# Rotary embedding of the first block's queries and keys: from a TensorE matmul to four VectorE operations, and an earlier place for four turns in its attention

## The chip, the cores and the metric

One core of one Trainium2 chip runs the whole program. The metric is the device time of one execution in microseconds (us), as the median of several runs. PE is TensorE, DVE is VectorE, ACT is ScalarE, POOL is GpSimd, and SP is the queue that loads weights.

## The reference, cut to what matters

The model has two blocks one behind the other. The change touches the first block only, which has two layers on 512 tokens. Each layer projects the normed input, rotates queries and keys, and runs three attention branches, a gated recurrence and a convolution beside each other:

```
q   = apply_rope(q.reshape(B, T, N_HEADS, HEAD_DIM), cos, sin)
k_c = apply_rope(kvr(k_c), cos, sin)      # likewise k_s and k_w
...
u1, u2 = jnp.split(uf, 2, axis=-1)        # the halves of a head: 32 and 32
out = jnp.concatenate([u1 * cos - u2 * sin, u2 * cos + u1 * sin], axis=-1)
```

## The kernel before, in words

Activations lie with features on the 128 partitions and the 512 tokens in the free dimension. A projection is a list of strips. A strip makes 128 output features: 8 chunks of the input times 128x128 weights, each chunk as three matmuls of a high and a low part (`three`, L949 to L951), into one PSUM bank. Strips use two banks in turn, so strip n waits until DVE has emptied the bank of strip n-2 (`taken`).

Weights come by SP in pieces of four chunks. ACT rounds a piece to its high part (`split_to`, L1334), POOL subtracts to get the low part (L2452), and PE waits for that. ACT takes its instructions in a fixed order: for strip n it first splits the pieces of strips n+1 and n+2, as far as `last_of(n) + SPLIT_RING` allows (4 pieces on), and then does its work on strip n and on strip n-1 (`evac`, `side`).

Part B of each layer has the strips k_c, v_c, q0, q1, c00, q2, c01, q3, d0, k_s, c10, v_s, c11, k_w, d1, v_w, g, z0, z1, z2 in this order; z3 is run inside the attention that follows. The c and d strips are the small matrices that compress keys and values (62 columns). Their weights are not split, and a c strip has 4 pieces, so ACT splits the weights of the strip behind it only when it comes to the c strip itself, and by then it has done `side` of the strip two before the c strip. So the weights of q2 (behind c00) wait for ACT's copy of the rotated q0, those of q3 (behind c01) for that of q1, and those of v_s (behind c10) for that of q3. Those of k_s are split at q3, behind ACT's copy of the rotated q2.

The seven strips k_c, q0 to q3, k_s and k_w of each layer (14 in all) are rotated. DVE scales the bank by the norm into a buffer (L1773, `evac`). PE multiplies the buffer by the constant matrix `rot`, which swaps the halves of each head and negates one (L1068, `rotate`, into bank 3). DVE multiplies that by the sines (L1990), the buffer by the cosines (L1995) and adds both (L1997). ACT copies the sum to its high part (L1476), and DVE subtracts to get the low part (L2001). For k_c DVE builds the blocks to be compressed instead (L2051). Between these DVE does the taps of the convolution (L2234), a fixed number behind each strip (`TAPS`).

In the attention NSA that follows, tiles come in pairs (two heads), two pairs make a group, and step s does on PE: the scores of group s (`scores`, L1161 and L1167), the values of group s-2 (`values`, L1198 and L1201), and the turns (transposes) of the probabilities of group s-1 (`turn`, L1188). POOL has scaled these probabilities before, and ACT or DVE copies each turned tile out of PSUM (L1540, L2123). The 9 pairs of one head column add up in bank 6. The first pair of the next column may start only when DVE has taken bank 6 (`output`, L2132). Pairs 9 and 27 of the 36 of a layer are the first of a column and the second of their group.

Of the kernel before, what the change touches and what calls it, by code (L numbers as in the profile page):

```python
# [22 lines left out]
ALU = mybir.AluOpType  # L23
# [3 lines left out]
P = 128  # L27
T = 512
NT = T // P
# [3 lines left out]
HD = 64  # L33
N_CMP = 31
CMP_PAD = 32
# [177 lines left out]
N_PARAM = _at  # L213


CONSTS = [("ident", P), ("ones", P), ("halves", P), ("rot", P), ("causal", T), ("cmp_mask", NT * CMP_PAD), ("cmp_any", 1), ("inv_freq", 1)]
EXTRA = [("rotc", P), ("band", 384), ("cos2d", T), ("sin2d", T), ("cos1d", T), ("sin1d", T), ("cosc", T), ("sinc", T),
         ("colmask", GRID)]
CONST_AT, EXTRA_AT = {}, {}
# [9 lines left out]
def build(nc, stream, x_in, mem_in, pos_in, par_in, const_in, extra_in, lruw_in, bias_in, out, counts):  # L229
# [5 lines left out]
    with ExitStack() as ctx:  # L235
# [43 lines left out]
        sin_t = sb("sin_t", [P, T])  # L279
# [31 lines left out]
        def C(name):  # L311
            a, w = CONST_AT[name]
            return consts[:, a:a + w]
# [5 lines left out]
        ident = C("ident")  # L319
# [200 lines left out]
        def rope_units(s):  # L520

            if s.kind in ("q", "qn"):
                return [(C("rot") if s.kind == "q" else None, s.idx)]
            if s.kind in ("k_s", "kn"):
                return [(C("rot") if s.kind == "k_s" else None, 4)]
            if s.kind in ("qr", "kr"):
                return [(None, 5 + s.idx if s.kind == "qr" else 9)]
            if s.kind == "k_w":
                return [(C("rot"), 5)]
            if s.kind == "k_c":  # L530
                return [(C("rot"), "cmp")]
            if s.kind == "uq":
                return [(extra("rotc"), ("latent", s.idx))]
            if s.kind == "krope":
                return [(extra("rotc"), "krope")]
            return []
# [149 lines left out]
        def in_group(groups, s):  # L686
            return groups[s] if 0 <= s < len(groups) else []
# [98 lines left out]
        def RAW(n):  # L786

            return raws[n % 4] if STRIPS[n].part[0] == "AB" else raw[n % 2]
# [157 lines left out]
        def _(pe):  # L946
# [110 lines left out]
            def rotate(n):  # L1057
                s = STRIPS[n]
                for u in s.units:
                    rot, _ = UNITS[u]  # L1060
                    if rot is None:
                        continue

                    pe.wait_ge(*after("latent_raw" if s.kind == "uq" else "strip_taken", n))
                    if u >= 1:

                        pe.wait_ge(*after("rope_taken", u - 1))
                    pe.matmul(bank[3][:, :], rot, rope_src(s), start=True, stop=True).then_inc(*mark("rotated", u))  # L1068
# [56 lines left out]
            def attend(part):  # L1125
# [102 lines left out]
                for s in range(steps_of(part)):  # L1228
                    if part[0] == "C2" and s < len(groups):
                        latent_scores(groups[s])  # L1230
                    else:
                        for pair in in_group(groups, s):
                            scores(pair)
                    if part[0] == "NSA" and s + 1 < len(GATE_CHUNKS):
                        for _ in range(GATE_CHUNKS[s + 1]):
                            next(begun[LAST_GATE[part[1]]])
                    if 0 <= s - len(groups) < 3:
                        drain(part, steps[s - len(groups)])
                    if PAIRS[part[0]] == 2:
                        for pair in in_group(groups, s - value_lag):  # L1240
                            values(pair)
                    for pair in in_group(groups, s - turn_lag):
                        for t in pair:
                            turn(t)
                    if PAIRS[part[0]] == 1:
                        for pair in in_group(groups, s - value_lag):
                            values(pair)
                    for i in moments_of(part, s):
                        for stage in between.get(i, ()):
                            extra_stage(*stage)  # L1250
# [426 lines left out]
        def _(dve):  # L1677
# [296 lines left out]
            def rope(n):  # L1974

                s = STRIPS[n]
                for u in s.units:
                    dst = UNITS[u][1]
                    src, swap = RAW(n), UNITS[u][0] is None
                    dve.wait_ge(*after(f"swapped{u % 2}" if swap else "rotated", u))  # L1980
                    turned, rt = (swapped[u % 2], swapped[u % 2]) if swap else (bank[3], tmp(2))
                    table = {"qn": "2d", "kn": "2d", "qr": "1d", "kr": "1d", "krope": "c"}.get(s.kind)
                    cos, sin = tables_of(s)
                    if table is not None:

                        dve.wait_ge(*after("tables_in_" + table, "sin"))
                        if table == "2d":
                            dve.wait_ge(*after("extra_in", "colmask"))
                    to = rr2[s.idx] if s.kind == "uq" else rr if dst != "krope" else krb
                    ins = dve.tensor_tensor(rt[:, :], turned[:, :], sin[:, :], ALU.mult)  # L1990
                    if s.kind == "uq":
                        ins.then_inc(*mark("rope_taken", u))
                    else:
                        settle(ins)
                        dve.tensor_tensor(to[:, :], src[:, :], cos[:, :], ALU.mult).then_inc(*mark("rope_taken", u))  # L1995
                    dve.wait_ge(*after("rope_taken", u))
                    dve.tensor_tensor(to[:, :], to[:, :], rt[:, :], ALU.add).then_inc(*mark("roped", u))  # L1997
                    dve.wait_ge(*after("roped", u))
                    if isinstance(dst, int):
                        dve.wait_ge(*after("roped_high", u))  # L2000
                        settle(dve.tensor_tensor(side_lo[:, dst, :], rr, side_hi[:, dst, :].bitcast(F32), ALU.subtract))  # L2001
                    elif dst == "cmp":
                        cmp_blocks(s.layer, 0)
# [465 lines left out]
def shape_constants():  # L2469

    f = np.float32
    d = np.arange(P)
    swap_sign = np.where(d % HD < 32, -1, 1).astype(f)[:, None]
    rot = np.zeros((P, P), f)
    for o in range(P):
        rot[o + 32 if o % HD < 32 else o - 32, o] = -1 if o % HD < 32 else 1
    q, x = d[:, None], np.arange(T)[None, :]
    n = np.arange(CMP_PAD)[None, None, :]
    t = (P * np.arange(NT))[None, :, None] + d[:, None, None]
    named = dict(  # L2480
        ident=np.eye(P, dtype=f), ones=np.ones((P, P), f), halves=(d[:, None] // HD == d[None, :] // HD).astype(f),
        rot=rot,
        causal=np.where(x - 384 <= q, 0, NEG).astype(f),
        cmp_mask=np.where((n < N_CMP) & (S_CMP * n + L_CMP - 1 <= t), 0, NEG).astype(f).reshape(P, -1),
        cmp_any=(d[:, None] >= L_CMP - 1).astype(f),
        inv_freq=(f(10000.0) ** (-(2 * (d % 32)).astype(f) / f(HD))).astype(f)[:, None],
    )
    pos = np.arange(T)
    inv64 = (f(10000.0) ** (-np.arange(0, 64, 2, dtype=f) / f(64))).astype(f)
    inv32 = (f(10000.0) ** (-np.arange(0, 32, 2, dtype=f) / f(32))).astype(f)  # L2490
    a1 = pos.astype(f)[None, :] * inv64[d % 32][:, None]
    fr = d % 32
    a2 = np.where(fr[:, None] < 16, (pos // GRID)[None, :], (pos % GRID)[None, :]).astype(f) * inv32[fr % 16][:, None]
    ac = pos[None, :].astype(f) * inv32[d % 16][:, None]
    rotc = np.zeros((P, P), f)
    for o in range(P):
        rotc[o + 16 if o % 32 < 16 else o - 16, o] = -1 if o % 32 < 16 else 1
    near = []
    for i in (0, 1):
        qc, kc = near_columns(i)  # L2500
        c0 = np.clip(qc - SPAN // 2, 0, GRID - SPAN)[SPAN // 2 * (d // GRID) + d % (SPAN // 2)][:, None]
        near.append(np.where((kc[None, :] >= c0) & (kc[None, :] < c0 + SPAN), 0, NEG))
    xb = np.arange(384)[None, :]
    extra = dict(rotc=rotc, band=np.where(np.abs(xb - P - q) <= 128, 0, NEG).astype(f),
                 cos2d=np.cos(a2).astype(f), sin2d=(swap_sign * np.sin(a2)).astype(f), cos1d=np.cos(a1).astype(f), sin1d=(swap_sign * np.sin(a1)).astype(f),
                 cosc=np.cos(ac).astype(f), sinc=np.sin(ac).astype(f),
                 colmask=np.concatenate(near, 1).astype(f))
    return (np.concatenate([named[k] for k, _ in CONSTS], 1), np.concatenate([extra[k] for k, _ in EXTRA], 1))

# [115 lines left out]
```

## Time and profile before

| What | us |
|---|---|
| Three runs: median (lowest to highest) | 2230.45 (2222.82 to 2232.63) |
| The profiled execution: its own time | 2232.77 |
| The profiled execution: span from the first to the last instruction | 2231.0 |
| PE busy in the span | 2151.1 |
| DVE busy | 1182.0 |
| ACT busy | 1014.1 |
| POOL busy | 1023.5 |

The span leaves 1.8 us of the execution's own time outside. Busy times are averages over stages with different limits. The mean granted clock of TensorE is 0.988 of its full speed.

### The profile page before, as it was taken

The numbers are of one execution on the slowest core, as the hardware profiler recorded it, in microseconds if no ns is written. First come the engines' busy times: TensorE is split into PE (matmuls) and PEld (weight loads), VectorE is DVE, ScalarE is ACT, GpSimd is POOL, SyncE is SP. The second block draws the span as 40 slices with busy tenths as digits, with TensorE's granted clock in tenths as the row PEclk, the third lists the DMA queues.
The fourth block names the chain that finished last, engine by engine and source line by source line (L and its number), as shares of the span: only waits on it lengthen the run. The fifth ranks groups of instructions, "written<-read, shape, count | busy, mean of one in ns | idle before, by whom it ended". The sixth has DMA issues, their size and how long they took to land.

```text
span 2231.0 us, 32894 instructions
## 1 busy us (share of the span) xinstructions
PE 2151.1 (96%) x11928; PEld 1747.1 (78%) x11928; DVE 1182.0 (53%) x2470; ACT 1014.1 (45%) x2020; POOL 1023.5 (46%) x937
## 2 busy tenths in 40 slices
PE   8999989999998899999999999999989999999997
PEld 6778767887876788768888888888757878888886
DVE  5997664389876546785562212234466654211222
ACT  6542455466246553585453323333356554322332
POOL 4433455444246544354345545554345525554553
PEclk9999989999999999999999999999999999999998
DMA  5334102333320233203233333333120413333332
GB/s 167 87 93 138 29 11 67 104 91 93 126 64 7 67 86 110 71 21 89 84 89 96 94 111 97 92 102 123 40 61 28 132 46 104 95 95 99 99 94 67
DMA packets 106895, 187.87 MB, mean 84 GB/s; under 512 B 12016, under 2 KB 22768, under 8 KB 106608
## 3 DMA queue, kind: packets, MB, share of 16 engines
q1 hardware_dynamic: 101136, 178.67, 27.7%
q10 hardware_dynamic: 5600, 7.11, 1.0%
q8 instruction: 97, 1.59, 0.3%
q14 instruction: 62, 0.51, 0.1%
HBM read 181.01 MB, written 2.10 MB: 82 GB/s over the span
## 4 chain that ended last, share of the span: by engine, by line
PE 86%; DVE 7%; ACT 2%; issue 2%; POOL 2%; DMA 0%; SPq 0%; DVEq 0%; ACTq 0%
PE bank L949 24%; PE bank L951 23%; PE bank L950 23%; PE bank L1188 4%; PE bank L1201 3%; PE bank L1167 2%; DVE bank L2234 1%; PE bank L956 1%; POOL temp L2406 1%; PE bank L1019 1%; PE bank L1146 1%; POOL w_lo L2452 1%; ACT temp L1529 1%; PE bank L1068 1%; PE bank L977 0%
## 5 line engine op out<-in xcount | busy, mean ns | idle before, releaser
L2452 POOL TENSOR_TENSOR w_lo<-w_raw,w_hi 128x512 fp32r<-128x512 f32 (+3 forms) x618 | 823.7, 1339 | 976.7 <-ACT w_hi L1334 976.5
L949 PE MATMUL bank<-op_hi,w_hi 128*128 128x512 f32 x1840 | 732.5, 398 | 11.5 <-POOL w_lo L2452 4.6
L951 PE MATMUL bank<-op_hi,w_lo 128*128 128x512 f32 x1840 | 719.5, 391 | 0.0
L950 PE MATMUL bank<-op_lo,w_hi 128*128 128x512 f32 x1840 | 719.2, 391 | 0.0
L1334 ACT ACTIVATE w_hi<-w_raw 128x512 fp32r<-128x512 f32 (+2 forms) x634 | 385.5, 617 | 685.1 <-PE bank L951 681.7
L949 PEld LDWEIGHTS bank<-op_hi,w_hi 128*128 128x128 f32 x1840 | 347.0, 189 | 96.0 <-issue 15.7
L950 PEld LDWEIGHTS bank<-op_lo,w_hi 128*128 128x128 f32 x1840 | 347.2, 189 | 74.0 <-issue 4.1
L951 PEld LDWEIGHTS bank<-op_hi,w_lo 128*128 128x128 f32 x1840 | 346.9, 189 | 73.1
L1773 DVE TENSOR_TENSOR temp<-bank,rstd 128x512 f32<-128x512 f32 x139 | 96.1, 691 | 368.4 <-PE bank L951 350.8
L949 PE MATMUL bank<-side_hi,w_hi 128*128 128x512 f32 (+1 forms) x628 | 233.1, 371 | 2.6 <-DVE side_lo L1872 1.4
L951 PE MATMUL bank<-side_hi,w_lo 128*128 128x512 f32 (+1 forms) x628 | 230.9, 368 | 0.0
L950 PE MATMUL bank<-side_lo,w_hi 128*128 128x512 f32 (+1 forms) x628 | 230.8, 368 | 0.0
L1854 DVE TENSOR_TENSOR x_t<-bank,x_t 128x512 f32<-128x512 f32 x80 | 55.3, 691 | 315.8 <-PE bank L951 315.6
L1529 ACT ACTIVATE temp<-temp,small 128x256 f32<-128x256 f32 (+3 forms) x288 | 166.2, 579 | 41.7 <-DVE small L2076 24.7
L2234 DVE SCALAR_TENSOR_TENSOR bank<-conv_area,par,bank 128x512 f32<-128x512 f32 x232 | 174.9, 754 | 6.8
L1188 PE MATMUL bank<-consts,temp 128*128 128x128 f32 x800 | 127.7, 285 | 31.6 <-POOL temp L2406 8.4
L1188 PEld LDWEIGHTS bank<-consts,temp 128*128 128x128 f32 x800 | 86.3, 142 | 71.6 <-issue 35.8
L949 PEld LDWEIGHTS bank<-side_hi,w_hi 128*128 128x128 f32 x628 | 118.4, 189 | 24.9 <-DVE side_lo L1872 2.7
L950 PEld LDWEIGHTS bank<-side_lo,w_hi 128*128 128x128 f32 x628 | 118.4, 189 | 19.5 <-issue 0.5
L951 PEld LDWEIGHTS bank<-side_hi,w_lo 128*128 128x128 f32 x628 | 118.4, 189 | 19.5
L2408 POOL TENSOR_SCALAR temp<-temp,small,consts 128x512 f32<-128x512 f32 (+2 forms) x128 | 85.2, 680 | 101.7 <-DVE small L2100 101.6
L2406 POOL TENSOR_SCALAR temp<-temp,small,gates 128x128 f32<-128x128 f32 (+3 forms) x128 | 76.6, 613 | 62.0 <-DVE small L2100 62.0
(286 smaller groups left out, 2431.7 us busy)
## 6 DMA issues: line engine op xcount, KB each, us to landing
w_raw<-in_weights SPq DMA_DIRECT2D x620, 256.0 KB, 2.7
w_raw<-in_weights SPq DMA_DIRECT2D x32, 192.0 KB, 2.3
temp<-temp SPq DMA_DIRECT2D x40, 64.0 KB, 2.0
x_t<-in_x SPq DMA_DIRECT2D x8, 256.0 KB, 5.3
conv_area<-in_mem ACTq DMA_DIRECT2D x2, 1024.0 KB, 5.4
conv_area<-in_bias ACTq DMA_DIRECT2D x1, 2048.0 KB, 7.6
out_y<-ybuf SPq DMA_DIRECT2D x8, 256.0 KB, 2.1
w_raw<-in_weights SPq DMA_DIRECT2D x10, 128.0 KB, 2.1
```

Of the source, the lines that this page charges most:

```text
L949: pe.matmul(dst, w[0], m[0], start=start, stop=False)
L950: pe.matmul(dst, w[0], m[1], start=False, stop=False)
L951: return pe.matmul(dst, w[1], m[0], start=False, stop=stop)
L1188: ins = pe.transpose(bank[t["turn"]][:, P * b:P * b + P], E[a % E_RING][:, P * b:P * b + P], ident)
L1201: ins = pe.matmul(dst, t["pv"][b], PT[a % PT_RING][:, P * b:P * b + P], start=t["start"] and b == 0, stop=t["stop"] and last)
L1334: act.activation(w_hi[:, j, 0:m * w], w_raw[:, p % RAW_RING, 0:m * w], ACT.Copy).then_inc(*mark("weights_high", p))
L1529: act.activation(e, e, ACT.Exp, bias=m, scale=-1.0, accum_out=total).then_inc(*mark("exps", a))
L1773: return dve.tensor_tensor(dst, strip_bank(n)[0:rows, 0:s.cols], f[0:rows, 0:s.cols], ALU.mult)
L2234: settle(dve.scalar_tensor_tensor(out=acc[:, c, :] if j == CONV_K - 1 else run, in0=u_conv[:, c, j:j + T], scalar=w, in1=run, op0=ALU.mult ...
L2406: ins = pool.tensor_scalar(e, e, total[:, r:r + 1], t["gate"], ALU.mult, ALU.mult)
L2408: ins = pool.tensor_scalar(e, e, total[:, r:r + 1], C("ones")[:, 0:1], ALU.mult, ALU.mult)
L2452: pool.tensor_tensor(w_lo[:, j, 0:n], w_raw[:, p % RAW_RING, 0:n], w_hi[:, j, 0:n].bitcast(F32), ALU.subtract).then_inc(*mark("weights_spl ...
```

## The change

Part one: the 14 rotations of part B leave PE. DVE multiplies by the sines itself, in four operations of 32 rows that read the other half of the head; its wait for PE is gone, and the matrix `rot` (128 columns of the constants, loaded at the start) is gone too. The products are the same numbers. The rotations of the second block stay as they were.

Part two: in NSA, where the second pair of a group is the first of a head column (pairs 9 and 27, so twice in a layer), PE does all four turns of the next group between the values of the first pair and those of the second, and not behind both.

```diff
-CONSTS = [("ident", P), ("ones", P), ("halves", P), ("rot", P), ("causal", T), ...
+CONSTS = [("ident", P), ("ones", P), ("halves", P), ("causal", T), ...
...
@@ rotate (PE)
-                    if rot is None:
+                    if rot is None or s.part[0] == "B":
                         continue
...
@@ attend (PE)
+                    to_turn = [t for pair in in_group(groups, s - turn_lag) for t in pair]
                     if PAIRS[part[0]] == 2:
-                        for pair in in_group(groups, s - value_lag):
+                        for i, pair in enumerate(in_group(groups, s - value_lag)):
+                            if part[0] == "NSA" and i == 1 and pair[0]["first"]:
+                                while to_turn:
+                                    turn(to_turn.pop(0))
                             values(pair)
-                    for pair in in_group(groups, s - turn_lag):
-                        for t in pair:
-                            turn(t)
+                    for t in to_turn:
+                        turn(t)
...
@@ rope (DVE)
-                    src, swap = RAW(n), UNITS[u][0] is None
-                    dve.wait_ge(*after(f"swapped{u % 2}" if swap else "rotated", u))
+                    src, swap, by_rows = RAW(n), UNITS[u][0] is None, s.part[0] == "B"
+                    if not by_rows:
+                        dve.wait_ge(*after(f"swapped{u % 2}" if swap else "rotated", u))
...
-                    ins = dve.tensor_tensor(rt[:, :], turned[:, :], sin[:, :], ALU.mult)
+                    if by_rows:
+                        for a in range(0, P, HD):
+                            low_rows, high_rows = slice(a, a + 32), slice(a + 32, a + HD)
+                            dve.scalar_tensor_tensor(out=rt[low_rows, :], in0=src[high_rows, :], scalar=-1.0, in1=sin_t[high_rows, :], op0=ALU.mult, op1=ALU.mult)
+                            ins = dve.tensor_tensor(rt[high_rows, :], src[low_rows, :], sin_t[low_rows, :], ALU.mult)
+                    else:
+                        ins = dve.tensor_tensor(rt[:, :], turned[:, :], sin[:, :], ALU.mult)
```

## Rows read from the trace of the kernel before

**Rows 1.** The page: busy time by engine, its share of the span, instructions.
```profile
PE 2151.1 (96%) x11928; PEld 1747.1 (78%) x11928; DVE 1182.0 (53%) x2470; ACT 1014.1 (45%) x2020; POOL 1023.5 (46%) x937
```

**Rows 2.** Windows: part B behind v_c in both layers (PE, PEld, DVE, ACT, POOL).
```profile
148.70:240.00 91.30, 89.51 (x453) 72.86 (x451) 74.46 (x122) 24.00 (x40) 29.44 (x23) 1.00 0.39 119
555.86:647.20 91.34, 89.48 (x453) 72.87 (x451) 74.42 (x121) 24.00 (x40) 29.44 (x23) 1.00 0.39 118
```

**Rows 3.** The rotation's line (two records each), and PE's timeline around the first.
```profile
L1068 PE MATMUL bank<-temp,consts x28: 590/592/697, 148.7 to 617.4; 128*128 128x512 f32 x28
...
148.25 0.39 PE L950 MATMUL bank<-op_lo,w_hi 128*128 128x512 f32 x1
148.47 0.39 PE L951 MATMUL bank<-op_hi,w_lo 128*128 128x512 f32 x1
...
149.80 0.40 PE L950 MATMUL bank<-op_lo,w_hi 128*128 128x512 f32 x1
```

**Rows 4.** Timeline of all engines from the end of q1 to q2.
```profile
160.76 0.69 DVE L1773 TENSOR_TENSOR temp<-bank,rstd 128x512 f32<-128x512 f32 x1 [0.42 <-PE bank L951]
...
161.55 0.69 DVE L1990 TENSOR_TENSOR temp<-bank,sin_t 128x512 f32<-128x512 f32 x1
162.27 0.69 DVE L1995 TENSOR_TENSOR temp<-temp,cos_t 128x512 f32<-128x512 f32 x1
...
163.72 0.63 ACT L1476 ACTIVATE side_hi<-temp 128x512 fp32r<-128x512 f32 x1 [14.13 <-DVE temp L1997]
164.26 1.13 ACT L1334 ACTIVATE w_hi<-w_raw 128x512 fp32r<-128x512 f32 x2
...
166.42 0.47 PE L949 MATMUL bank<-op_hi,w_hi 128*128 128x512 f32 x1 [0.48 <-POOL w_lo L2452]
```

**Rows 5.** DVE's timeline: a strip of 24 rows, and three operations with no wait between.
```profile
222.35 0.68 DVE L1773 TENSOR_TENSOR temp<-bank,rstd 24x512 f32<-24x512 f32 x1
...
546.52 0.68 DVE L2018 TENSOR_TENSOR temp<-bank,temp 128x512 f32<-128x512 f32 x1
547.11 0.69 DVE L2019 SCALAR_TENSOR_TENSOR bank<-temp,bank 128x512 f32<-128x512 f32 x1
```

**Rows 6.** DVE's timeline: operations on 64 rows without a wait, in overlapping windows.
```profile
152.27 0.58 DVE L2051 TENSOR_TENSOR temp<-temp,par 64x248 f32<-64x248 f32 x1
152.77 1.15 DVE L2051 TENSOR_TENSOR temp<-temp,par 64x248 f32<-64x248 f32 x2
153.35 1.06 DVE L2051 TENSOR_TENSOR temp<-temp,par 64x248 f32<-64x248 f32 x2
```

**Rows 7.** Timeline: DVE's slack at q2 and q3, ACT's splits for k_s and v_s.
```profile
172.25 0.69 DVE L1773 TENSOR_TENSOR temp<-bank,rstd 128x512 f32<-128x512 f32 x1 [0.96 <-PE bank L951]
...
179.65 1.14 ACT L1334 ACTIVATE w_hi<-w_raw 128x512 fp32r<-128x512 f32 x2
...
182.17 0.69 DVE L1773 TENSOR_TENSOR temp<-bank,rstd 128x512 f32<-128x512 f32 x1 [1.63 <-PE bank L951]
...
191.00 1.13 ACT L1334 ACTIVATE w_hi<-w_raw 128x512 fp32r<-128x512 f32 x2
```

**Rows 8.** PE's timeline where NSA's first head column ends, and DVE's output.
```profile
276.73 0.61 PE L1201 MATMUL bank<-temp,vz 128*64 128x128 f32 x8
...
277.41 0.69 DVE L2132 TENSOR_TENSOR ybuf<-bank,ybuf 128x512 f32<-128x512 f32 x1 [0.25 <-PE bank L1201]
...
278.20 0.29 PE L1198 MATMUL bank<-temp,vcz 128*64 128x128 f32 x1 [0.87 <-issue]
...
280.30 0.45 PE L1167 MATMUL bank<-side_hi 64*128 64x384 f32 x2
```

**Rows 9.** Timeline: a wait of PE; windows behind it (the clock third from last).
```profile
326.98 2.13 PE L1188 MATMUL bank<-consts,temp 128*128 128x128 f32 x10 [2.52 <-POOL temp L2406]
...
329.00:330.00 1.00, 1.00 (x9) 0.95 (x10) 0.58 (x5) 0.98 (x5) 0.32 (x1) 0.50 0.00 0
...
331.00:332.00 1.00, 1.00 (x14) 1.00 (x12) 0.28 (x2) 0.16 (x2) 0.88 (x2) 0.59 0.00 0
```

More of the change, by code:

```diff
@@ L213 @@
 N_PARAM = _at
-CONSTS = [("ident", P), ("ones", P), ("halves", P), ("rot", P), ("causal", T), ("cmp_mask", NT * CMP_PAD), ("cmp_any", 1), ("inv_freq", 1)]
+CONSTS = [("ident", P), ("ones", P), ("halves", P), ("causal", T), ("cmp_mask", NT * CMP_PAD), ("cmp_any", 1), ("inv_freq", 1)]
 EXTRA = [("rotc", P), ("band", 384), ("cos2d", T), ("sin2d", T), ("cos1d", T), ("sin1d", T), ("cosc", T), ("sinc", T),
@@ L522, in rope_units @@
             if s.kind in ("q", "qn"):
-                return [(C("rot") if s.kind == "q" else None, s.idx)]
+                return [("rows" if s.kind == "q" else None, s.idx)]
             if s.kind in ("k_s", "kn"):
-                return [(C("rot") if s.kind == "k_s" else None, 4)]
+                return [("rows" if s.kind == "k_s" else None, 4)]
             if s.kind in ("qr", "kr"):
@@ L528, in rope_units @@
             if s.kind == "k_w":
-                return [(C("rot"), 5)]
+                return [("rows", 5)]
             if s.kind == "k_c":
-                return [(C("rot"), "cmp")]
+                return [("rows", "cmp")]
             if s.kind == "uq":
@@ L2473, in shape_constants @@
     swap_sign = np.where(d % HD < 32, -1, 1).astype(f)[:, None]
-    rot = np.zeros((P, P), f)
-    for o in range(P):
-        rot[o + 32 if o % HD < 32 else o - 32, o] = -1 if o % HD < 32 else 1
     q, x = d[:, None], np.arange(T)[None, :]
@@ L2481, in shape_constants @@
         ident=np.eye(P, dtype=f), ones=np.ones((P, P), f), halves=(d[:, None] // HD == d[None, :] // HD).astype(f),
-        rot=rot,
         causal=np.where(x - 384 <= q, 0, NEG).astype(f),
```

## The prediction

> **What bounds the kernel now.** I read the page first. PE is busy for 96% of the span, DVE for 53% [rows 1]. By that reading work should go from PE to DVE. But these are averages, so I took the windows of part B, where the 14 rotations are: DVE works 74.5 of 91.3 us there and PE 89.5 [rows 2]. Both layers have the same picture within 0.1 us. DVE has 17 us free in a layer, and the next question is where.
>
> The timeline shows it [rows 4]. DVE waits 0.42 us for q1 to end (160.76), rotates q0 from 161.55, and ACT, which had been idle for 14.13 us because the next instruction in its fixed order is the copy of the rotated q0, makes the copy at 163.72. Only then does it split the weights of q2 (164.26). POOL makes the low part, and PE starts q2 at 166.42, after a wait for it. So behind a c strip the rotation on DVE is what PE waits for: DVE, ACT, POOL, PE in a chain. The same chain leads from the rotated q2 to the weights of k_s (split at 179.65) and from q3 to those of v_s (191.00) [rows 7]. Ahead of q2 DVE has almost no free time.
>
> **What leaves PE.** A rotation is two records of 592 ns that overlap. Between the last L951 before it and the second matmul of the next strip lie 149.80 - 148.47 = 1.33 us, where two steps of 0.23 us would be 0.45 [rows 3]. So it costs 0.88 us, and 14 are 12.3 us. That is the gain if PE sets the pace.
>
> **What comes to DVE.** L1990 takes a step of 162.27 - 161.55 = 0.72 us [rows 4]. Four operations of 32 rows take its place. Fewer rows save nothing: 24 rows by 512 take 0.68 us, as 128 rows do [rows 5]. The negating form with a number for its scalar (L2019) takes 0.69 us too. No row before has two inputs from SBUF in that form; I take 0.69 us and leave 0.76 us as a bound.
>
> The step from one operation to the next is in doubt. Where nothing is waited for it can be 547.11 - 546.52 = 0.59 us, 0.09 less than the duration [rows 5]. In L2051 the steps are 0.50 and then 0.58 us, at durations of 0.56 to 0.58 [rows 6]. The 0.50 lies between two operations on the same rows; the 0.58 comes where the output changes to the other 64 rows. In the new series the rows of input and output change at every operation. By the first rows the four take 3 x 0.60 + 0.72 = 2.52 us, so 1.80 us more than now; by the second 3 x 0.70 + 0.72 = 2.82 us, 2.10 more. I take 2.10, since L2051 is the nearer row, and keep 1.80 and, for contention or a slower form, 2.40 as bounds.
>
> The Trainium skill (VectorE: DVE Perf Modes, Two Vector instructions with no wait between them) says that a Vector instruction whose input or output starts in another group of 32 partitions than the one before is held until all earlier ones have finished. By it the series takes the longer step; L2051 agrees.
>
> **The walk through part B (layer 0; layer 1 has the same steps).** I follow how late each thing is. Up to q2 two rotations (k_c, q0) add 2 x 2.10 = 4.2 us. DVE saves 0.1 us twice, where it now waits for L1068 behind the scaling, and the 0.42 us wait for PE is used up. So ACT's copy and q2 are 3.6 us late (170.0). PE had gained 1.75 us by then (two rotations) and stands idle for 6 to 7 us.
>
> The rotation of q1 adds 2.2; DVE's slack of 0.96 us at q2 [rows 7] goes; the scaling of q2 is 4.8 late. The rotation of q2 adds 2.2, and the split for k_s is 7.0 late. k_s began 2 us after its weights were ready, so it is 5.0 late. Ahead of q3's scaling DVE had 1.63 us free [rows 7]; the rotation of q3 adds 2.1; the split for v_s is 7.5 late and v_s itself 6.9, after 0.6 us of its own slack. From here on the gains and losses on PE count. The rotation of k_w goes (0.88 less). DVE, some 8 us late by then with the rotations of k_s and k_w, delays the strips behind it by up to 0.6 us. Then it has time to catch up (few taps, no rotation). So z2 and the end of part B are 6.7 us late in each layer. With 1.80 for 2.10 the walk gives 4.9, with 2.40 it gives 8.4. The same walk without the new costs comes within 1.1 us of the starts in the trace, at every strip.
>
> The idle time before q2 may cost more. Behind the wait of 2.52 us that ends at 326.98 the granted clock is 0.50 at 329 and 0.59 in the window from 331, and full before and behind [rows 9]: about 3.3 us at the lower level (1.2 GHz), which lose 1.6 us. If q2 runs so, the scaling of q2 waits for PE, which adds 0.4 us in the walk; k_s has cover, because DVE is later still. I add 0.4 in each layer. Part one in all: 2 x 7.1 = +14.2 us.
>
> The shorter constants (64 KB at the start) I cost at nothing: the first strips run on other transfers.
>
> **Part two.** After the last values of the column (about 277.3) PE waits for DVE's output (277.41 to 278.10), does the values of the next pair from 278.20, then two turns with a wait for a copy, and reaches the next scores at 280.30 [rows 8]. With the turns first, two of them fill the wait; the third needs ACT's copy of the first, the fourth DVE's copy of the second, which comes behind the output: 278.1 + 0.3 = 278.4. The values then run from 278.6 to 279.5 and the scores start at 279.6, 0.7 us sooner. In the other place of the layer the wait is also 0.87 us. Four places give 2.8 us at most; nothing is the lower bound. I take 2.8: the turns also release DVE's and ACT's copies. What is queued behind the earlier turns is the pair's values; ACT's third copy waits for them, and they come sooner as well.
>
> **Sum.** 14.2 - 2.8 = +11.4 us. Against the profiled execution 2232.77 + 11.4 = 2244.2. That execution lies 2.3 us above the median of the runs, so for the median 2230.45 + 11.4 = 2241.9, say 2242. About 0.5% (11.2 us) is what a measurement of this kernel can tell from no change; the forecast lies on that edge.
>
> **The rivals.**
> - *Shorter steps on DVE* (1.80 us a rotation, or slack that the walk doesn't see): 2 x 4.9 - 2.8 = +7, so 2237. For it: three operations at 0.60 us [rows 5]. Against it: rows change here. Chance 0.25.
> - *PE's clock.* PE will stand idle ahead of q2 (about 6.9 us), k_s (about 3 to 4) and v_s (1 to 3). If the lower level holds for 6 us and not 3.3, q2 loses 3 us and passes 1.5 of it on; if v_s too runs slowly, there is no cover and 1.6 us or more go straight to the end. That makes 8.9 to 11 us a layer, less 2.8: +15 to +19, so 2246 to 2250. For it: the longest idle time is more than twice that of [rows 9]. Chance 0.25. The Trainium skill (TensorE: Matmul & The Clock Gate, Part 1) says that the array's clock is granted by how busy it has lately been and falls to half after idling; the windows agree, and by it each long gap is paid for.
> - *The rotation is hidden and PE sets the pace* (the other side): DVE's 17 us of free time in a layer [rows 2] would swallow 7 x 2.1 = 14.7. Then 12.3 + 2.8 = 15 us are gained, 2215. It decides for this one if ACT's copy is not in front of the splits; the wait of 14.13 us that ends with DVE's add [rows 4] speaks against it. Half of it, with delays only ahead of q2, would be about 2226. Chance 0.05.
> - *The turns gain nothing* (POOL's scaling or DVE is late instead): +14, so 2244.5; this one lies within the forecast's own range.
>
> **The numbers.** The forecast has 0.45, with a range of its own from 2239 to 2246. The cases below and above it have 0.25 each, the hidden rotation 0.05. The range 2231 to 2250 leaves out the last and the worst of the clock. Slower by over 0.5% (above 2241.6): the upper half of the forecast (0.26) and the clock (0.24), 0.50. Faster by over 0.5% (below 2219.3): 0.03. The rest is 0.47.
>
> **What would show it.** In the profile after: no L1068 on the constants in part B; in its place 56 operations of 32x512 with a mean near 690 ns and starts 0.70 us apart (0.60: the second case). PE's wait for w_lo before q2 grows from 0.48 to 6 or 7 us, and new ones stand before k_s and v_s. The windows of part B are 6 to 8 us longer in each layer with DVE at nearly the same share. The granted clock behind q2's start tells the third case. In NSA, L1198 has no wait of 0.87 us in two of its places in a layer, and four L1188 stand before it. I am wrong if q2 starts sooner than 168, or if part B is not longer.

## The result, and the profile after

The changed kernel takes 2247.78 us (median of four runs, 2247.19 to 2249.88). The kernel before, run beside it, took 2229.34 us (four runs, 2222.82 to 2232.63). The ratio is 1.0093, with a 95% interval from 1.0076 to 1.0109. So the change costs 18.4 us where 11.4 were forecast. The direction held, and 2247.8 lies inside the wide range (2231 to 2250) but outside the forecast's own (2239 to 2246): 18.4 us lies where the rival of PE's clock stood (+15 to +19). The profiled execution took 2249.88 us, 17.1 more than that of before; its mean granted clock is 0.982, that of before 0.988.

The page first. PE lost 28 instructions and 5 us, DVE gained 42 and 33 us. The span grew all the same: PE is busy for less time in a longer span. This answers to [rows 1].

```profile
PE 2145.9 (95%) x11900; PEld 1745.9 (78%) x11900; DVE 1214.8 (54%) x2512; ACT 1013.3 (45%) x2020; POOL 1022.7 (45%) x937
```

The windows of part B behind v_c, from the same event to the same event as in [rows 2] (columns as there, the granted clock third from last):

```profile
148.51:251.42 102.91, 88.41 (x439) 73.75 (x437) 90.55 (x143) 23.55 (x40) 29.64 (x23) 0.92 0.35 105
561.71:664.43 102.72, 88.24 (x439) 73.72 (x437) 90.37 (x142) 23.54 (x40) 29.65 (x23) 0.92 0.36 105
```

Both layers grow, by 11.6 and 11.4 us. DVE now works 90.5 of 102.9 us, more than PE's 88.4. The clock was 1.00 here before and is 0.92 now.

The timeline of the first rotation (k_c) and of POOL. The four operations and then the two behind them:

```profile
149.49 1.29 POOL L2462 TENSOR_TENSOR w_lo<-w_raw,w_hi 128x512 fp32r<-128x512 f32 x1 [1.43 <-ACT w_hi L1337]
149.51 1.81 DVE L1997 SCALAR_TENSOR_TENSOR temp<-temp,sin_t 32x512 f32<-32x512 f32 x1
...
151.34 0.68 DVE L1998 TENSOR_TENSOR temp<-temp,sin_t 32x512 f32<-32x512 f32 x1
...
152.03 0.69 DVE L1997 SCALAR_TENSOR_TENSOR temp<-temp,sin_t 32x512 f32<-32x512 f32 x1
```

The first operation takes 1.81 us, where the others take 0.69. It starts 0.02 us behind an operation of POOL and ends 0.54 us after that one's end (151.32 against 150.78). Its line and the line of the 64-row operations, in part B of layer 0, show one such long operation each (durations in ns: shortest, median, longest):

```profile
L1997 DVE SCALAR_TENSOR_TENSOR temp<-temp,sin_t x14: 679/686/1814, 149.5 to 228.2; 32x512 f32<-32x512 f32 x14
...
L2061 DVE TENSOR_TENSOR temp<-temp,par x16: 561/572/1550, 154.9 to 194.5; 64x248 f32<-64x248 f32 x16
```

In the kernel before, the same view has a longest of 583 ns for the 64-row line, and one operation in L1995 of 1024 ns (median 692). So 1.13 and 0.98 us come in and 0.33 go, in both layers alike. The first of the second series of eight 64-row operations is long too, by 0.27 us, and it lies beside POOL as well:

```profile
188.72 2.79 POOL L2462 TENSOR_TENSOR w_lo<-w_raw,w_hi 128x512 fp32r<-128x512 f32 x2 [8.61 <-ACT w_hi L1337]
189.56 0.84 DVE L2061 TENSOR_TENSOR temp<-temp,par 64x248 f32<-64x248 f32 x1
```

That series takes 5.56 us in all, and took 4.29: the chain loses 1.27 us there, not 0.98.

Next the stretch that answers to [rows 4], from the rotation of q0 to q2:

```profile
163.72 0.68 DVE L1997 SCALAR_TENSOR_TENSOR temp<-temp,sin_t 32x512 f32<-32x512 f32 x1
164.41 0.68 DVE L1998 TENSOR_TENSOR temp<-temp,sin_t 32x512 f32<-32x512 f32 x1
165.10 0.69 DVE L1997 SCALAR_TENSOR_TENSOR temp<-temp,sin_t 32x512 f32<-32x512 f32 x1
165.80 0.68 DVE L1998 TENSOR_TENSOR temp<-temp,sin_t 32x512 f32<-32x512 f32 x1
166.52 0.69 DVE L2005 TENSOR_TENSOR temp<-temp,cos_t 128x512 f32<-128x512 f32 x1
...
167.97 0.63 ACT L1479 ACTIVATE side_hi<-temp 128x512 fp32r<-128x512 f32 x1 [18.57 <-DVE temp L2007]
168.51 1.13 ACT L1337 ACTIVATE w_hi<-w_raw 128x512 fp32r<-128x512 f32 x2
...
170.67 0.77 PE L949 MATMUL bank<-op_hi,w_hi 128*128 128x512 f32 x1 [6.91 <-POOL w_lo L2462]
171.23 0.63 PE L950 MATMUL bank<-op_lo,w_hi 128*128 128x512 f32 x1
```

The starts lie 0.69 and 0.70 us apart. The chain DVE, ACT, POOL, PE is there as before, and PE waits 6.91 us. The second matmul of q2 takes 0.63 us, not 0.39. The two other waits that the walk foresaw, at k_s and at v_s:

```profile
190.19 0.47 PE L949 MATMUL bank<-op_hi,w_hi 128*128 128x512 f32 x1 [2.42 <-POOL w_lo L2462]
...
203.30 0.77 PE L949 MATMUL bank<-op_hi,w_hi 128*128 128x512 f32 x1 [3.90 <-POOL w_lo L2462]
```

And the windows around q2 and v_s. The clock falls while PE stands idle and is at the lower level (1.2 GHz) when the strip begins:

```profile
164.00:166.00 2.00, 0.00 (x0) 0.00 (x0) 1.96 (x4) 0.00 (x0) 0.00 (x0) 0.65 0.85 289
166.00:168.00 2.00, 0.00 (x0) 0.00 (x0) 1.87 (x3) 0.03 (x1) 0.00 (x0) 0.50 0.05 17
...
172.00:174.00 2.00, 2.00 (x6) 1.55 (x5) 1.94 (x4) 0.26 (x1) 0.00 (x0) 0.50 0.49 176
174.00:176.00 2.00, 2.00 (x8) 1.61 (x8) 1.92 (x4) 0.00 (x0) 0.00 (x0) 0.79 0.00 0
...
204.00:206.00 2.00, 2.00 (x7) 1.52 (x6) 1.91 (x5) 0.26 (x1) 0.38 (x1) 0.50 0.60 183
206.00:208.00 2.00, 2.00 (x6) 1.61 (x5) 1.94 (x3) 0.00 (x0) 0.00 (x0) 0.50 0.04 13
208.00:210.00 2.00, 2.00 (x8) 1.53 (x8) 1.21 (x2) 1.25 (x3) 0.02 (x1) 0.76 0.00 0
```

Summed over windows of 1 us, 17.1 us of part B run at the lower level in each layer, and none did before.

Last, the place in NSA that answers to [rows 8]: four transposes now stand ahead of the pair's values, and the wait of 0.87 us is gone.

```profile
287.02 0.44 PE L1188 MATMUL bank<-consts,temp 128*128 128x128 f32 x2
287.17 0.69 DVE L2142 TENSOR_TENSOR ybuf<-bank,ybuf 128x512 f32<-128x512 f32 x1 [0.24 <-PE bank L1201]
...
287.72 0.72 PE L1188 MATMUL bank<-consts,temp 128*128 128x128 f32 x2 [0.26 <-POOL temp L2416]
...
288.37 0.32 PE L1198 MATMUL bank<-temp,vcz 128*64 128x128 f32 x1
...
289.39 0.45 PE L1167 MATMUL bank<-side_hi 64*128 64x384 f32 x2
```

From the output's start to the next scores it takes 289.39 - 287.17 = 2.22 us, and took 280.30 - 277.41 = 2.89.

**Where the 17.1 us of the profiled executions lie.** Part B holds +23.0. From its end to the first output residual behind NSA the changed kernel is 5.5 us shorter in layer 0 and 1.5 in layer 1 (-7.0): in NSA of layer 0 the kernel before had 20.5 us at the lower level, the changed one 10.2. The block behind has +1.3 (one stretch at the lower level that before lacks). So nearly all of the cost is in part B. Layer 1, where both kernels have 10.2 us at the lower level in NSA, shows what the turns give without the clock: 1.5 us. The rest of the 5.5 us in layer 0 is the clock.

### The profile page after: what moved, and what is told of

It is laid out like the page before. It is cut to its first block, busy times and chain, and to the rows that moved or that the text cites. A ratio compares the mean times of both kernels' runs of the same rounds, so it can differ in the third digit from the quotient of the medians.

```text
span 2248.1 us, 32865 instructions
## 1 busy us (share of the span) xinstructions
PE 2145.9 (95%) x11900; PEld 1745.9 (78%) x11900; DVE 1214.8 (54%) x2512; ACT 1013.3 (45%) x2020; POOL 1022.7 (45%) x937
## 4 chain that ended last, share of the span: by engine, by line
PE 84%; DVE 9%; ACT 2%; issue 2%; POOL 1%; DMA 0%; SPq 0%; DVEq 0%; ACTq 0%
PE bank L949 23%; PE bank L951 23%; PE bank L950 23%; PE bank L1188 4%; PE bank L1201 3%; PE bank L1167 2%; DVE bank L2244 1%; PE bank L956 1%; DVE temp L2061 1%; POOL temp L2416 1%; PE bank L1146 1%; DVE temp L1997 1%; DVE temp L1998 0%; DVE temp L1776 0%; DVE temp L2005 0%
```

## The experiments

To compare runs without the clock's chance elsewhere, I measured one stretch of each trace: from the start of DVE's scaling of v_c to that of z2, in layer 0. It is 90.75 us in the kernel before and 102.36 in the changed one. The last column names what PE waits for only where it isn't the low part of the weights.

| Kernel | Stretch | At the lower level in part B, layer 0 | Wait of PE at q2, k_s, v_s |
|---|---|---|---|
| before | 90.75 | 0 | 0.48, none, none |
| changed | 102.36 | 17.1 | 6.91, 2.42, 3.90 |
| e1, rows alone | 101.64 | 17.1 | 6.91, 2.42, 2.25 |
| e2, turns alone | 90.73 | 0 | as before |
| e3, two gaps filled | 99.86 | 6.8 | 1.70, 3.71, none |
| e4, splits ahead | 102.82 | 17.1 | none, 2.78, 2.89 (both for DVE) |
| e5, all on rows 0 to 31 | 99.80 | 13.6 | 6.50, 2.02, 3.61 |
| e6, k_c by PE | 98.25 | 10.3 | 4.26, 2.42, 2.26 |
| e7, only k_s and k_w by rows | 89.34 | 0 | 0.48, none, none |
| e8, three gaps filled | 99.03 | 0 | 1.70, 1.06, 2.11 |

### The two parts by themselves

e1 is the changed kernel with the turns back in their old place. e2 is the kernel before with the turns moved:

```diff
+                    to_turn = [t for pair in in_group(groups, s - turn_lag) for t in pair]
...
+                            if part[0] == "NSA" and i == 1 and pair[0]["first"]:
+                                while to_turn:
+                                    turn(to_turn.pop(0))
```

> The rotations by rows alone, the turns as before. Theory 1 (VectorE's longer rotation sets the starts of q2, k_s and v_s, and the clock falls in the gaps): part B 11.5 us longer in each layer as in the changed kernel, in all +19 to +23 us against the kernel before, so slower than the changed kernel by the 3 us of the turns. Rival: the loss comes partly from the moved turns (copies held up in the ring); then this run is less slow than the changed kernel, +15 or less.

> The moved turns alone, rotations on TensorE. Theory 1: -0.7 us at each of four places, -2.8 us in all (-0.13%), possibly 1.7 us more or less where a stretch at the lower clock moves. Rival (the turns gain nothing, or hold up the values): 0 to +3 us.

Measured (before: 2228.93, 15 runs): e1 2251.55 us, ratio 1.0102 (1.0088 to 1.0117); e2 2229.18 us, ratio 0.9998 (0.9989 to 1.0007). The rows are the whole loss. By the medians the turns alone give nothing. But the mean granted clock of e2's eleven runs is 0.9884, that of before 0.9899. At the same clock e2 is shorter: at 0.988 2229.49 against 2232.36 us (four runs each), at 0.989 2226.98 (four) against 2230.78 (three). So at one clock the turns give 2.9 to 3.8 us, and the clock took it back. e1 says the same: it lacks only the turns, its mean clock is that of the changed kernel (0.983), and it takes 3.8 us longer. e10 below tests it again.

### The clock: idle matmuls in PE's gaps

e3 fills PE's waits behind c00 and c10, e8 also the one behind the second product of the compressed keys, ahead of k_s. The matmuls write a bank that nobody reads.

```diff
+                        if STRIPS[n].kind == "cmp2" and STRIPS[n].idx in (0, (0,)):
+                            warm(3, 3)
+                        if STRIPS[n].kind == "cmp1":
+                            warm(3, {(0, 0): 6, (1, 0): 2}.get(STRIPS[n].idx, 0))
```

This is e8. e3 has the last two lines alone, with 6 and 3. The numbers say how many matmuls stand in each gap.

> The changed kernel with idle matmuls on TensorE behind c00 (6) and c10 (3) of each layer, into a bank that nobody reads, so that the gaps ahead of q2 and v_s are filled. Theory 1 with the clock: q2 starts when it did (170.7), the clock stays full, q2 no longer passes 0.7 us on and v_s no longer loses 2.8 us: 3.5 us a layer, 7 us in all below the changed kernel. Rival (the clock costs nothing because VectorE is later still): no change within 2 us, and the excess of part B over the walk is VectorE's own.

> The changed kernel with idle matmuls of TensorE in all three gaps (six behind c00, three behind the second product of the compressed keys ahead of k_s, two behind c10). The matmuls compute nothing. If what is left above the walk of 7 us a layer is the clock, no stretch at the lower level stands behind q2, k_s or v_s, and the time falls a further 2 to 5 us below that with two gaps filled: 2239 to 2242. If VectorE's lateness alone sets the strips, filling the third gap changes nothing: 2243 to 2245.

Measured: e3 2243.93 us, ratio 1.0070 (1.0056 to 1.0084). e8 2245.02 us beside a before of 2227.00, ratio 1.0077 (1.0061 to 1.0094). Both are a few us shorter than the changed kernel (ratio 1.0093), and both miss: e3 should have gained 7 us and gains 3.9, e8 should have come to 2239 to 2242 and be below e3. By the time alone e8 fits the rival, that DVE's lateness sets everything. The traces tell why. In e3 the clock fell at the gap ahead of k_s that I had left open. PE reaches it sooner and waits 3.71 us there; in the changed kernel it waits 2.42 us and the clock doesn't fall:

```profile
188.01 0.77 PE L949 MATMUL bank<-op_hi,w_hi 128*128 128x512 f32 x1 [3.71 <-POOL w_lo L2464]
```

```profile
186.00:188.00 2.00, 0.00 (x0) 0.02 (x1) 1.92 (x3) 0.98 (x2) 1.46 (x2) 0.56 0.17 64
188.00:190.00 2.00, 1.99 (x5) 1.61 (x6) 1.99 (x3) 0.00 (x0) 1.32 (x1) 0.50 0.32 122
```

In e8 nothing of part B runs at the lower level, in either layer. This is the whole of part B, from the same events as above:

```profile
148.51:248.17 99.66, 93.51 (x462) 74.13 (x460) 90.62 (x143) 23.53 (x40) 29.70 (x23) 1.00 0.36 109
```

```profile
170.75 0.47 PE L949 MATMUL bank<-op_hi,w_hi 128*128 128x512 f32 x1 [1.70 <-POOL w_lo L2466]
...
189.62 0.47 PE L949 MATMUL bank<-op_hi,w_hi 128*128 128x512 f32 x1 [1.06 <-POOL w_lo L2466]
...
202.74 0.47 PE L949 MATMUL bank<-op_hi,w_hi 128*128 128x512 f32 x1 [2.11 <-POOL w_lo L2466]
```

The strips still start late (q2 21.9 us behind the scaling of v_c in both), so the idle matmuls took nothing from the chain. What is left, 99.03 - 90.75 = 8.3 us a layer, is the cost without the clock. The clock's share in the changed kernel is 102.36 - 99.03 = 3.3 us. It can be split: q2's own scaling, and with it k_s and v_s, come 0.65 us sooner in e8 (counted from the scaling of v_c, k_s starts at 40.76 and not 41.41), and the other 2.7 us arise behind the start of v_s. What e8 gained in part B, it lost in part in NSA: 27.3 us at the lower level in both layers' NSA against 20.5 in the changed kernel.

### ACT's order

The prediction said that ACT is idle because the copy of the rotated strip stands ahead of the next split. e4 lets ACT split up to three strips ahead in part B.

```diff
+                        if step[1][0] == "B":
+                            split_ahead(n, most)
                         split_to(min(last_of(n + 2), last_of(n) + SPLIT_RING, most))
```

> The changed kernel, but ScalarE splits the weights of up to three strips ahead in part B, before it waits for the rotated strip. Theory 1 (the weights' split behind ScalarE's wait for the rotation is the link): the waits for w_lo ahead of q2, k_s and v_s go, part B gets back most of its 11.5 us; 2225 to 2232 in all. Rival (VectorE is saturated, 74.5 + 14.7 of 85 us, and the emptying of the banks sets the pace): the waits for w_lo turn into waits for VectorE's scaling, and no more than 8 us come back, 2240 or more.

Measured: 2252.29 us, ratio 1.0105 (1.0086 to 1.0123), no faster than the changed kernel. q2 does start sooner, at 167.36, without a wait. PE now waits for DVE's scaling instead:

```profile
162.04 5.56 PE L1019 MATMUL bank<-temp,w_raw 128*128 128x62 f32 x32 [2.35 <-DVE temp L1786]
...
180.59 0.61 PE L949 MATMUL bank<-op_hi,w_hi 128*128 128x512 f32 x1 [2.48 <-DVE temp L1786]
```

```profile
204.79 0.80 PE L949 MATMUL bank<-op_hi,w_hi 128*128 128x512 f32 x1 [2.89 <-DVE temp L1786]
```

So ACT's order is where the lateness enters PE in the changed kernel, but without it PE is late all the same. DVE is busy for 65.7 of the 72 us from 147 to 219, and whoever asks it next waits. My theory that this order is the binding link fell; the rival, a full DVE, holds for the most part. The run isn't a clean test, though: the earlier splits also move POOL's work. Seven DVE operations in this stretch take 1.4 to 1.8 us beside POOL, five of them ahead of v_s, which costs DVE 2.5 us more there than in the changed kernel. v_s starts only 1.35 us later (55.87 us behind the scaling of v_c, and 54.52). So the order may be worth about 1 us of v_s's lateness of 10 (an estimate from these numbers), and what it is worth behind v_s e4 can't show.

### The step between the operations

e5 lets all four operations read and write rows 0 to 31, into four buffers, so nothing changes rows. The rotated product is not computed.

```diff
-                            low_rows, high_rows = slice(a, a + 32), slice(a + 32, a + HD)
...
+                        rows = slice(0, 32)
+                        for one, other in ((rt, tmp(10)), (tmp(3), bank[3])):
```

> The four operations of a rotation all read and write rows 0 to 31, into four different buffers, so the output group of rows never changes and no operation has to see the result of the one before; the rotated product is not computed. If a change of rows holds an operation back until the one before has ended, the starts come 0.59 to 0.60 us apart instead of 0.69 to 0.70, a rotation is 0.3 us shorter, the four rotations ahead of v_s give 1 to 1.5 us a layer, and the kernel is 2 to 4 us shorter than the changed one (2244 to 2246). If the step is simply the duration, starts stay 0.69 to 0.70 apart and the time does not move.

Measured: 2242.61 us (four runs, one of them 2253.92 at a clock of 0.979; before 2227.00), ratio 1.0078 (1.0054 to 1.0101). The steps are 0.60 us:

```profile
163.44 0.67 DVE L1997 SCALAR_TENSOR_TENSOR temp<-temp,sin_t 32x512 f32<-32x512 f32 x1
164.04 0.67 DVE L1998 TENSOR_TENSOR temp<-temp,sin_t 32x512 f32<-32x512 f32 x1
164.64 0.67 DVE L1997 SCALAR_TENSOR_TENSOR temp<-temp,sin_t 32x512 f32<-32x512 f32 x1
165.24 0.68 DVE L1998 TENSOR_TENSOR bank<-temp,sin_t 32x512 f32<-32x512 f32 x1
```

Before v_s that makes 1.3 us a layer (v_s starts 53.2 us behind the scaling of v_c, in the changed kernel 54.5), and the stretch is 2.6 us shorter; most of the rest is the clock, which is at the lower level for 3.4 us less. So the kernel gains more than the 2 to 4 us that I expected. The same trace holds the answer to the long operations. At k_c the order of the two engines is turned round here:

```profile
149.66 0.67 DVE L1997 SCALAR_TENSOR_TENSOR temp<-temp,sin_t 32x512 f32<-32x512 f32 x1
149.75 1.74 POOL L2462 TENSOR_TENSOR w_lo<-w_raw,w_hi 128x512 fp32r<-128x512 f32 x1 [1.43 <-ACT w_hi L1337]
150.25 1.77 DVE L1998 TENSOR_TENSOR temp<-temp,sin_t 32x512 f32<-32x512 f32 x1
```

DVE began first; POOL's operation takes 1.74 us instead of 1.29, and the next one of DVE is held in its turn: it ends at 152.02, 0.53 us behind POOL's end (151.49). All the long operations seen (L1997, L1998, L2061, and L1995 before) have both inputs in SBUF; the L1990 that the change removes read one input from PSUM and was never among them (693 ns at most). The Trainium skill (SBUF — State Buffer, Who interferes with whom) says that a DVE instruction with two SBUF inputs contends with a GpSimd instruction that reads SBUF, that the ports they share are an exclusive lock, and that the order of issue decides who is blocked. The traces agree: a DVE operation that begins just behind one of POOL takes 0.98 to 1.13 us longer. No run removes these collisions and nothing else, so their price is read from the durations.

### Which rotations cost, and which are hidden

e6 gives k_c back to PE. e7 is the kernel before with the turns moved and k_s and k_w alone by rows.

```diff
-                    src, swap, by_rows = RAW(n), UNITS[u][0] is None, s.part[0] == "B"
+                    src, swap, by_rows = RAW(n), UNITS[u][0] is None, (s.part[0] == "B" and s.kind != "k_c")
```

This is e6; e7 has `s.kind in ("k_s", "k_w")` in its place. PE's side has the same condition in both, and `rot` is among the constants again.

> The changed kernel with k_c alone rotated by TensorE again, which takes VectorE's rows operation out of GpSimd's way at 149.5 and 2.1 us off VectorE ahead of q2. If VectorE's lateness and the collision set q2's start, TensorE's wait before q2 falls from 6.9 to about 3.2 us, each layer ends 2 to 4 us sooner and the time is 2240 to 2244. If what counts is only that TensorE idles long enough ahead of q2 for its granted clock to fall, a wait of 3 us costs the dip all the same and the time is 2245 to 2248. The dip itself can go too: then 2237 to 2240.

> The kernel before, with the turns moved and with the rotations of k_s and k_w alone by rows (k_c and the four q by TensorE as before). If VectorE's lateness counts only ahead of the strips c00 to v_s, these two rotations are covered, TensorE is 2 x 0.88 us shorter in each layer, and with the 2.9 us of the turns the kernel is 4 to 6 us faster at equal granted clock: 2223 to 2226, less if the clock takes some back as it did for the turns. If VectorE has no room there either, the rotations cost 1 to 2 us a layer and the time is 2229 to 2232.

Measured (before 2227.00): e6 2242.30 us, ratio 1.0062 (1.0047 to 1.0077). e7 2230.10, ratio 1.0005 (0.9992 to 1.0017). The time of e6 is the one that I expected from DVE's lateness (2240 to 2244), and its stretch is 4.1 us shorter than in the changed kernel. But the wait at q2 is 4.26 us, not the 3.2 that I expected; the clock still falls there, for 3.4 us instead of 10.2. By its time alone e7 lies in the range that I gave for "no room there either" (2229 to 2232). The trace says otherwise: its stretch is 1.4 us shorter than before, PE has no new wait, and of the 2 x 0.88 us that left PE 1.4 come through. So the price of a rotation on DVE depends on its place: nothing or nearly nothing behind v_s, all of it ahead. That the whole kernel isn't faster is again the clock: 0.9875 in the mean of e7's runs, 0.9910 in before's. At 0.991 e7 took 2223.08 (one run), before 2226.78 to 2228.74 (six runs).

### Holding the clock in the attention

This is the test of what e2 and e7 suggest. Idle matmuls of PE fill the entry of NSA and its two long waits: one of 1.87 us in layer 0 and 2.22 in layer 1, and the 2.52 us of [rows 9], which both layers have:

```diff
-WARM_TURN = {"NSA": {}, "AB2": {0: 2}, "D2": {0: 2}, "C2": {0: 2}, "X2": {0: 2}}
+WARM_TURN = {"NSA": {36: 2, 52: 2}, "AB2": {0: 2}, "D2": {0: 2}, "C2": {0: 2}, "X2": {0: 2}}
...
+                if part[0] == "NSA":
+                    warm(4, 1)
                 for s in range(steps_of(part)):
```

e9 has only this, e10 the turns besides, e11 the turns and the rotations of e7, and e12 is the changed kernel as in e8 with this.

> The kernel before, with idle matmuls of TensorE in the attention part of each layer: one at its entry, two ahead of the transposes that wait 1.9 us, two ahead of those that wait 2.5 us. They compute nothing. In the profiled execution of before, 20.5 us of the first attention part ran at the lower level and 10.2 us in the second layer. If these waits are what the clock falls for, about 15 of 27 us at the lower level go, the spread of the runs shrinks, and the kernel is 4 to 10 us faster: 2217 to 2223, clock 0.994 to 0.997. If the dips only move, the time stays within 2 us of before.

> The kernel before, with the turns moved and the same idle matmuls. If the turns gain what the timeline shows (2.8 to 2.9 us) and only the clock ate it, this one is 2 to 3.5 us faster than the kernel before with idle matmuls, at the same clock. If the turns gain nothing, the two are within 1 us.

> The turns moved, k_s and k_w alone rotated by rows, and the same idle matmuls. At equal clock the version without the idle matmuls was about 4.4 us faster than before, 1.5 us beyond the turns. If that holds, this one is 1 to 3.5 us faster than the turns with idle matmuls; if the rotations of k_s and k_w cost VectorE what they save TensorE, the two are within 1 us.

> The changed kernel with idle matmuls in its three gaps and in the attention parts, so that hardly any stretch at the lower level is left. What is left against the kernel before with idle matmuls is the cost of the change without the clock: by the walk and the collision with GpSimd, 2 x 8.2 us in part B less 2.8 us of the turns, so 12 to 15 us slower than that kernel. If VectorE's lateness is smaller than the walk says and the clock makes most of the difference, 5 to 9 us.

| Kernel | Median us (runs) | Ratio to before (2227.52, 23 runs) | Mean clock |
|---|---|---|---|
| e9, before held | 2227.16 (11) | 0.9995 (0.9982 to 1.0008) | 0.9925 |
| e10, turns held | 2223.19 (11) | 0.9980 (0.9970 to 0.9990) | 0.9928 |
| e11, late rows held | 2221.23 (7) | 0.9971 (0.9960 to 0.9982) | 0.9927 |
| e12, changed held | 2238.89 (5) | 1.0051 (1.0038 to 1.0063) | 0.9940 |

e9 misses what I expected (2217 to 2223). In its profiled execution the attention of layer 0 has no stretch at the lower level (the clock of these 140 us is 1.00, and 0.93 in the kernel before), and from z2's scaling to the first output residual it takes 123.2 us instead of 130.7. But over the eleven runs the mean clock rises only from 0.9907 to 0.9925, and at the same clock e9 is the longer one, by 1 to 1.6 us (0.994 and 0.992), which I put down to the idle matmuls. One profile shows one of many outcomes of the clock. The window of these 140 us in e9:

```profile
240.00:380.00 140.00, 127.86 (x1070) 98.62 (x1070) 83.31 (x269) 80.39 (x212) 77.35 (x99) 1.00 0.12 31
```

e10 is the answer for the turns. Its median is 4.0 us below that of e9 and its mean 3.2, at a mean clock that is nearly the same (0.9928 and 0.9925; the difference is worth about 0.5 us). Runs of equal clock differ by 1.8 us (0.994), 3.0 (0.993), 2.3 (0.992) and 4.8 (0.990), with one to five runs on a side. In the traces, the stretch from the third head column's output to the first output residual is 37.15 us in e10 and 38.08 in e9, without a fall of the clock in either. With the 0.67 us of the first place that is 1.6 us a layer, 3.2 in all. e11 is 2.0 us below e10 and 6.3 us below the kernel before; it beats both kernels, and nothing that it does is new beside the parts of this change but the idle matmuls. e12 is 11.7 us above e9, just under the 12 to 15 that I expected. It has a higher clock than e9, so at one clock the difference is larger: e9's two runs at 0.994 took 2222.93 and 2224.12, and e12 is 15.4 above their mean.

## Why the prediction came out as it did

**The chain held.** DVE, ACT, POOL, PE, with waits ahead of q2, k_s and v_s: 6.91 us ("6 to 7"), 2.42 ("3 to 4") and 3.90 ("1 to 3"): the first is in its range, the second below it, the third above. That a rotation is not hidden ahead of v_s was right (e1, e6), and so was the reading of DVE's 17 us of free time as being in the wrong place. e7 shows where that place is. e4 corrects the wording: a full DVE is the main cause, and ACT's order hands it on.

**The step of 0.70 us held.** 28 operations of L1998 have a median of 683 ns, the starts are 0.69 to 0.70 us apart, and the rival of shorter steps was wrong here; e5 shows that it would be right on the same rows (0.60). Fewer rows save nothing: also right.

**The walk was too short by 1.6 us a layer.** It gave 6.7 us, and e8 measures 8.3 with the clock at its upper level. The term that is missing is the one that I kept as "contention" only in the bound of 2.40 us a rotation: DVE operations that are held by POOL, 1.13 us at k_c and 1.27 in the second series of L2061, less the 0.33 that before had, so 2.1 us on the chain. The first is ahead of q2 (forecast 3.6 us late, measured 4.4, each counted from the scaling of v_c), the second ahead of v_s. There the starts must be compared at the second matmul, since PE's rotation stood right before the first one and delayed the step to the second:

```profile
192.88 1.08 PE L1068 MATMUL bank<-temp,consts 128*128 128x512 f32 x2
193.39 0.80 PE L949 MATMUL bank<-op_hi,w_hi 128*128 128x512 f32 x1
194.03 0.40 PE L950 MATMUL bank<-op_lo,w_hi 128*128 128x512 f32 x1
```

That is 45.06 us behind the scaling of v_c in the kernel before. In e8 it is 54.19 (203.05 - 148.86), so 9.1 us late where the walk had 6.9; 2.1 of the 2.2 us are the held operations. Behind v_s the walk added up to 0.6 us for a late DVE that the run doesn't show: from 9.1 us PE's saved 0.88 at k_w leads to the 8.3.

**The clock was the large error.** I allowed 0.4 us a layer; it costs 3.3 (e8 against the changed kernel). The step that failed is the clock's term: it priced only the gap before q2 and gave the gap before v_s no loss. In the trace 10.2 us are at the lower level around q2 and 6.8 around v_s, where PE itself works at half speed for some 4.2 and 5.6 us and so loses 2.1 and 2.8. At q2 the length was wrong ("about 3.3 us at the lower level", taken from [rows 9], though the wait is nearly three times as long), but the price was nearly right: DVE's lateness covers most of the 2.1 us, and 0.65 pass on where 0.4 were allowed. At v_s nothing covers the loss, as the rival said, and 2.7 us a layer go to the end. The rival's range (+15 to +19) held the result, though with other terms: 1.5 us at q2 and 1.6 or more at v_s. The rule of the Trainium skill that stood beside it, that each long gap is paid for, held for the clock at q2 and v_s, though the gap at q2 was paid for by PE more than by the kernel.

**The turns held as a term (2.8 us).** Runs of equal clock give 2.9 and 3.8 us (e2) and 1.8 to 4.8 (e10 against e9), and the traces 0.67 us at the place of [rows 8], where 0.7 was forecast, and 0.93 at the other place of the layer.

**The sum again.** 2 x 8.3 for part B, 2 x 3.3 for its clock, less 3 for the turns, are 20.2 us. Against the forecast 5.8 of these are the clock's term and 3.2 the walk's. The profiled executions differ by 17.1; the rest is the clock outside part B, where the changed kernel happened to lose some 2 to 3 us less. The medians differ by 18.4. Had the clock outside part B been the same in both, the cost would have been about 20 us, above the rival's range too; that it lies inside is in part luck.

## What to carry to other kernels

Before work moves to an engine that is half idle, read its idle time in the stretch ahead of the next consumer, not in the stage: the same rotation cost 2.1 us and more ahead of v_s and next to nothing behind it. Look where the moved operation's inputs lie: one that read PSUM and now reads two operands from SBUF can be held behind GpSimd. And price each new gap of TensorE with the clock that follows it, the last one above all: a slow stretch is covered only where the work behind it waits for something else anyway.

## What the runs showed of the hardware

- Time follows the mean granted clock closely. Over 23 runs of the kernel before, 0.988 goes with 2232.4 us (three runs), 0.991 with 2226.1 to 2228.4 (eleven), 0.994 with 2222.6: about 1.6 us for 0.001. This is nearly the whole spread of a kernel on one core, and it can hide a gain of 3 us (e2).
- A version with a shorter schedule can have the lower mean clock. e2 and e7 have a mean of 0.9884 and 0.9875 beside 0.9899 and 0.9910 of before. I did not find out whether this is the emptier schedule or only a shift of the waits in time.
- The same gap doesn't always cost the same. A wait of 2.42 us at k_s kept the upper level in the changed kernel and cost 3.4 us of the lower in e1 and in e6; in the kernel before, a wait of 1.87 us in NSA of layer 0 was followed by 3.4 us too, and the one of 2.22 us at the same place of layer 1 by none. The periods at the lower level came as 3.4, 6.8 or 10.2 us.
- DVE and POOL hold each other up, mostly by 0.98 to 1.13 us on DVE's side and 0.45 on POOL's (e5), where POOL reads SBUF and the DVE operation has both inputs there. A held DVE operation of 32 or 128 rows ended 0.53 to 0.55 us behind POOL's (e4 has the 0.55).
